# Moving the partner features of a rotary embedding between partitions by DMA instead of by a TensorE product

## The reference, cut to what matters

```
kh = axial_rope(rms_norm_2(kb..., g_knorm), ang_row, ang_col)
qh = axial_rope(rms_norm_2(qb..., g_qnorm), ang_row, ang_col)

def rotate(x, ang):                    # on each half of the 128 features
    x1, x2 = x[..., :m], x[..., m:]    # m = 32
    return concatenate([x1 * cos - x2 * sin, x2 * cos + x1 * sin])
```

## Time and profile before

| what | value |
|---|---|
| median of 3 runs | 3807.99 us (3806.25 to 3811.59) |
| profiled execution, its own time | 3809.24 us |
| its span | 3807.1 us |
| PE busy | 3518.0 us (92% of the span) |
| DVE, ACT, POOL busy | 1419.5, 991.5, 781.9 us |
| preparation of heads, group 0 | about 2371 to 2471 us of the span |
| preparation of heads, group 1 | about 2671 to 2774 us of the span |

### The profile page before, as it was taken

The page is one execution under the profiler, slowest core; times in us unless marked ns, Lnnn a source line. Parts: engine busy times, 40 slices in busy tenths (PEclk is TensorE's granted clock), DMA queues, the critical chain, the costliest instruction groups (busy, mean ns, idle before and its releaser), DMA issues.

```text
span 3807.1 us, 54098 instructions
## 1 busy us (share of the span) xinstructions
PE 3518.0 (92%) x20966; PEld 3032.4 (80%) x20966; DVE 1419.5 (37%) x2330; ACT 991.5 (26%) x1723; POOL 781.9 (21%) x515
## 2 busy tenths in 40 slices
PE   8999988999999989999999999899999999699996
PEld 6666766888887868888888899777777999489996
DVE  3454343000004545555555520645555133511212
ACT  3232241000001224444444410244144211311112
POOL 3112203232322332111111132100100122012121
PEclk9999989999999999999999999999999999799998
DMA  3001112111112120000000011100000121468786
GB/s 144 23 22 33 33 56 78 50 44 50 44 49 89 50 84 18 17 19 25 17 17 17 11 42 58 68 1 11 23 1 11 55 90 56 157 232 274 267 271 220
DMA packets 69590, 268.89 MB, mean 71 GB/s; under 512 B 9249, under 2 KB 9889, under 8 KB 68753
## 3 DMA queue, kind: packets, MB, share of 16 engines
q1 hardware_dynamic: 62304, 228.81, 17.3%
q0 software_dynamic: 5632, 17.05, 2.0%
q10 hardware_dynamic: 1584, 22.07, 1.4%
HBM read 229.55 MB, written 38.34 MB: 70 GB/s over the span
## 4 chain that ended last, share of the span: by engine, by line
PE 54%; DVE 4%; issue 2%; ACT 1%; DMA 0%; POOL 0%; ACTq 0%; DVEq 0%; POOLq 0%; SPq 0%
PE PS L511 23%; PE PS L499 6%; PE PS L2207 6%; PE PS L2096 4%; PE PS L2215 3%; PE PS L1950 3%; PE PS L1909 3%; PE PS L2075 3%; PE PS L2097 1%; PE PS L1951 1%; DVE EA L1586 1%; PE PS L2019 1%; PE PS L2062 1%; PE PS L2024 0%; PE PS L1922 0%
## 5 line engine op out<-in xcount | busy, mean ns | idle before, releaser
L511 PE MATMUL PS<-u_hi,w_hi 128*128 128x512 f32 (+1 forms) x2464 | 661.4, 363 | 39.9 <-DVE u_lo L465 11.5
L511 PE MATMUL PS<-u_lo,w_hi 128*128 128x512 f32 (+1 forms) x2464 | 653.5, 360 | 0.0
L511 PE MATMUL PS<-u_hi,w_lo 128*128 128x512 f32 (+1 forms) x2464 | 648.7, 358 | 0.0
L533 POOL CAST w_hi<-ring 128x1024 fp32r<-128x1024 f32 x174 | 183.0, 1052 | 1805.0 <-PE PS L511 1608.9
L511 PEld LDWEIGHTS PS<-u_hi,w_hi 128*128 128x128 f32 x2464 | 439.0, 190 | 114.5 <-issue 51.5
L511 PEld LDWEIGHTS PS<-u_hi,w_lo 128*128 128x128 f32 x2464 | 441.6, 189 | 57.1
L511 PEld LDWEIGHTS PS<-u_lo,w_hi 128*128 128x128 f32 x2464 | 443.0, 189 | 54.1
L535 POOL TENSOR_TENSOR w_lo<-ring,w_hi 128x1024 fp32r<-128x1024 f32 x174 | 419.6, 2411 | 14.0
L904 DVE TENSOR_TENSOR hid<-sq,PS 128x1024 f32 x22 | 26.9, 1221 | 457.9 <-PE PS L511 457.9
L1349 ACT ACTIVATE EA<-EA,small_sb 128x1040 f32<-128x1040 f32 x144 | 166.4, 1155 | 90.2 <-DVE small_sb L1586 90.1
L1586 DVE CUSTOM_DVE_ANT_0 EA<-PS,biasH,low_a 128x1024 f32<-128x1024 f32 x128 | 163.4, 1281 | 25.8 <-PE PS L1909 25.1
(11 more groups left out here) (332 smaller groups left out, 5274.3 us busy)
## 6 DMA issues: line engine op xcount, KB each, us to landing
ring<-in_stream SPq DMA_DIRECT2D x174, 512.0 KB, 3.5
w_gate_sb<-in_w_gate SPq DMA_DIRECT2D x64, 512.0 KB, 3.9
w_up_sb<-in_w_up SPq DMA_DIRECT2D x64, 512.0 KB, 7.1
w_down_sb<-in_w_down SPq DMA_DIRECT2D x64, 512.0 KB
x_keep<-xT ACTq DMA_DIRECT2D x2, 4176.0 KB, 13.0
xT<-x_keep ACTq DMA_DIRECT2D x1, 4176.0 KB, 12.9
x2T<-x_keep ACTq DMA_DIRECT2D x1, 4176.0 KB, 14.0
x_keep<-x2T SPq DMA_DIRECT2D x1, 4176.0 KB, 13.8
```

The costliest lines, as they stand in the source:

```text
L511: last = mm(bank(to_bank, width), w[j][:, c, :], src[:, c, b * width:(b + 1) * width], start=(c == 0 and k == 0), stop=(c == KD - 1 and k ...
L533: pool.tensor_copy(w_hi[j][:, :, :], w_raw[j][:, :, :]).then_inc(S["w_rounded"], 1)
```

## The change

The permutation matrix `swap`, its load and its product are gone. In their place ACT starts four DMAs a head, SBUF to SBUF, 32 partitions by 1040 floats (130 KB) each, which write the partner rows of `raw_b` straight into `swapped`. The sign that `swap` carried is now in the table `sin`.

- ACT starts them behind the square of the head, when `raw_b` is written and DVE has finished the last product of the head before (`ob_q`), which is the last reader of `swapped`. The wait stands in ACT's program ahead of `root(n)` and `raw(n+1)`.
- `ob_sw` now counts the landed DMAs (64 a head). DVE's product with the sine waits for it, and is one instruction on 1040 elements from SBUF instead of three from PSUM. `raw(n)` waits for it as before.
- The waits on `ob_m2` that guarded the PSUM banks, ahead of the next projection and of the second square root, are gone.

```
-    swap = np.zeros((P, P), np.float32)
...
+    for first in (0, 64):
+        sin[first:first + 32] *= -1.0
...
-                sp.dma_start(swap[:, :], A["swap"]).then_inc(S["const_ld"], 16)
...
-                pe.wait_ge(S["const_ld"], 48)
+                pe.wait_ge(S["const_ld"], 32)
...
-                            act.wait_ge(S["ob_sw"], i)
+                            act.wait_ge(S["ob_sw"], 64 * i)
                         act.activation(thirds(raw_b[:, :]), banks(3 * (n % 2), 3, CH), ACT.Copy, scale=gain).then_inc(S["ob_raw"], 1)
                         act.activation(thirds(sq_b[:, :]), banks(3 * (n % 2), 3, CH), ACT.Square).then_inc(S["ob_sq"], 1)
+                        act.wait_ge(S["ob_raw"], i + 1)
+                        if i >= 1:
+                            act.wait_ge(S["ob_q"], i)
+                        for r in range(0, P, 32):
+                            act.dma_start(swapped[r:r + 32, :], raw_b[r ^ 32:(r ^ 32) + 32, 0:T2]).then_inc(S["ob_sw"], 16)
...
-                        act.wait_ge(S["ob_m2"], 3 * i + 3)
...
-                        dve.wait_ge(S["ob_sw"], i + 1)
-
-                        for k in range(3):
-                            w = min(CH, T2 - k * CH)
-                            c = slice(k * CH, k * CH + w)
-                            if i and k == 0:
-                                dve.wait_ge(S["ob_m3"], i)
-                            ins = dve.tensor_tensor(swapped[:, c], bank(3 * (n % 2) + k, w), sin[:, c], ALU.mult)
-                            ins.then_inc(S["ob_m2"], 1)
-                        dve.wait_ge(S["ob_m2"], 3 * i + 3)
+                        dve.wait_ge(S["ob_sw"], 64 * (i + 1))
+                        dve.tensor_tensor(swapped[:, :], swapped[:, :], sin[:, :], ALU.mult).then_inc(S["ob_m2"], 1)
+                        dve.wait_ge(S["ob_m2"], i + 1)
...
-                        for b in range(3):
-                            last = mm(bank(first + b, CH), swap[:, :], raw_b[:, b * CH:(b + 1) * CH], start=True, stop=True)
-                        last.then_inc(S["ob_sw"], 1)
...
-                            pe.wait_ge(S["ob_m2"], 3 * (i - 1))
...
-                    pe.wait_ge(S["ob_m2"], 3 * (z0 + GROUP))
```

More of the change, by code:

```diff
@@ L84, in host_constants @@
     block = np.kron(np.eye(2), np.ones((HD, HD))).astype(np.float32)
-    swap = np.zeros((P, P), np.float32)
-    for half in (0, 64):
-        for i in range(32):
-            swap[half + 32 + i, half + i] = -1.0
-            swap[half + i, half + 32 + i] = 1.0
     delta = np.arange(P)[:, None] - (np.arange(T1)[None, :] - (T1 - P))
@@ L108, in host_constants @@
     sin = np.sin(ang).astype(np.float32)
-    return {"eye": eye, "ones": ones, "block": block, "swap": swap, "log_count": log_count, "neg_dist": neg_dist,
+    for first in (0, 64):
+        sin[first:first + 32] *= -1.0
+    return {"eye": eye, "ones": ones, "block": block, "log_count": log_count, "neg_dist": neg_dist,
             "cos": cos, "sin": sin}
@@ L148, in build @@
         block64 = put("block_sb", [P, P])
-        swap = put("swap_sb", [P, P])
         gains = put("gains_sb", [P, GAINS])
```

## The result

| | before | changed |
|---|---|---|
| median, 20 runs each | 3808.19 us | 3825.80 us |
| lowest and highest run | 3795.05, 3821.36 | 3811.28, 3838.57 |
| ratio, with its 95% interval | | 1.0037 (1.0024 to 1.0051) |
| profiled execution, its own time | 3809.24 us | 3826.91 us |

The ratio times the time before is 14 us more; 10 less were forecast. Times in us.

What follows compares the result with a forecast made beforehand. PE was taken as the bound, with a 16.82 us head period and DVE's chain close at group ends. Gains of 4.7 and 5.7 us, 10.4 together, off the median of 3807.99 gave 3798 us, range 3795 to 3807.

Steps and rivals of the forecast that it cites:

- The product with `swap` off PE: In each pipeline head PE loses 1.85 us of matmul, so its period falls from 16.82 to 14.97 us.
- The issue: Four DMA starts on ACT, 0.48 us apart, hold ACT about 1.9 us a head, hidden behind PE's projection.
- The landing: L, from DVE's last product of one head to its next sine product: taken as 4.0 us, bounds 3.44 and 5.84.
- the prediction's own formula: Total gain is 10.4 - 2 x (L - 4.0) up to L = 4.47, then 9.5 - 8 x (L - 4.47).
- The rival of slow narrow transfers: 32-partition transfers at half rate, one after another: L = 5.3, gain 2.9, total 3805 us; chance 22%.
- the estimate of 4.8: L from the skill page's 189 GB/s: some 2.8 us plus a fixed 2, a gain near 7.
- DVE's cycle: Per head on DVE, L + 10.5 us, 14.5 at L = 4.0, so under PE's 14.97, which sets the pace.
- The sign that I had named for it: The forecast is wrong if DVE's reciprocal starts behind its own sum, as DVE's cycle is then the pace.
- The end of a group: Scores start 0.1 us behind `k_lo`, gaining 4.7 and 5.7 us in the two groups; PE idle 5 to 7 us before.
- PE's clock: Rival: longer idling ahead of the scores doubles the low-clock stretch there, losing 6.4 us in all; total 3804; chance 8%.
- The chances: Faster 0.60, same within 0.2% 0.33, slower 0.07.
- a late landing: Rival: DVE waits for the DMAs in every head; slower from L = 5.66 (10%), by over 0.2% from 6.6.

Runs made afterwards that it cites:

- a_dbl: The changed kernel with a second buffer for the partner rows, so a head's DMAs wait for the head before the last; 3808.52 us, ratio 0.9969 against before.
- a_poolwait: The changed kernel with POOL's split of the next weights held until DVE has made the sum; 3810.12 us, ratio 1.0001 against before.

## Why the prediction was wrong

- *The product with `swap` off PE.* Right in itself: 60 records gone. The pace of 14.97 us came only where DVE let it: 15.04 in a_dbl and 15.02 to 15.04 in a_poolwait.
- *The issue.* Taken as 0.48 us apiece, measured 0.54 to 0.64 (1.40 and 1.21 in the first four). Hidden on ACT's side, as forecast, but for 0.8 us in head 4: its copy waited for the landing of head 3's transfers, where PE was no longer waited for.
- *The landing.* Taken as 4.0, measured 4.28 to 4.33 in seven of eight intervals and 5.15 in the last of group 1, which cost the scores there some 0.8 us; why is not known. One transfer lands in 2.4 us (2.2 assumed from the 64 and 512 KB rows). By the prediction's own formula the 0.28 costs 0.6 us. The rival of slow narrow transfers (L = 5.3 in every head) is out, and so is the estimate of 4.8 from the Trainium skill's page SBUF — State Buffer, section "Door 1: The DMA port swizzle".
- *DVE's cycle.* This step failed in its size. I put three operations at 1.24 us each, from rows in which POOL was still. With L at 4.28 DVE's cycle was 14.8 and just under PE's; the stretch by POOL, 2.55 us in head 1 and 1.45 in head 2, made it the pace. a_poolwait takes this out: its preparations are 3.0 and 3.9 us shorter than the changed kernel's (the late landing in group 1, 0.8 us, did not come again there either), 6.9 of the 8.0 us by which the changed stage missed its forecast (a gain of 2.4 for 10.4; of 9.3 in a_poolwait). The sign that I had named for it, a reciprocal that starts behind its own sum and not behind the root, is in the period of the chain shown above.
- *The end of a group.* Right: the scores 0.11 us behind `k_lo`, PE idle for 5.45 and 7.55 us, where 5 to 7 were forecast.
- *PE's clock.* This step decided the result, and it failed in its place and its size. I gave the clock 8% and 6.4 us, at the scores alone. The row at the scores did become lower than in the earlier trace rows, 0.50 for 7 us, as that rival said:

```profile
2459.00:2466.00 7.00, 7.00 (x26) 6.25 (x27) 2.14 (x7) 0.00 (x0) 0.00 (x0) 0.50 0.00 0
```

  The rest fell in the 200 us of attention behind it, where I took the clock as fixed because nothing changed there. The term should have read: 52 us more at the low level, at 0.38, minus 20 us. What brings these 52 us about is open but for the pauses that they follow. The kernel before already showed how wide this can be: its 20 runs went from 3795 to 3821, almost three times my gain.
- *The chances.* "Slower" came from a late landing only, with 7%. A cost that can fall on any change that shifts a loop by a microsecond was in none of the cases. Nothing in the trace of before gave its sign, but it did show that the attention's time was not fixed: its two attentions run the same instructions and took 200.2 and 204.5 us, with 6.5 and 17 us at the low level.

## What to carry to other kernels

Where runs of one kernel scatter by 20 us or more with their mean clock, split every result into the time at full clock and the low-clock time, by a fit of span against clock over all runs, and hold the first against the stages, since low-clock time in which PE waits anyway costs nothing. A gain under 0.5% is hard to tell otherwise, and a few versions with a harmless shift of a microsecond show how much of a loss the clock can make by itself. A transfer that replaces matmuls needs its own buffer: with one buffer the landing and all that stretches DVE stand in the loop (up to 17.28 us a head here, 15.04 with two), and an operation that moves from PSUM to SBUF operands is to be priced beside what POOL does there.

## What the runs showed of the hardware

- A transfer from SBUF to SBUF of 32 partitions by 1040 floats (130 KB), on ACT's queue, landed in 2.4 us in the median (2.2 to 3.3, but 6.0 to 6.7 for the four that were started while the store of 4176 KB was under way); four that were started 0.6 us apart had landed 4.2 us after the first start in eight of nine cases, and 5.0 in the other.
- A DVE operation and a POOL operation that both read two SBUF operands of some 1000 elements took 3.30 and 3.25 us side by side; alone they took 1.24 and 2.4. The one that began later was the one drawn out: in a_poolwait DVE's cosine product began at 2675.44, 0.08 us ahead of POOL's subtraction, and took 1.24 us, POOL's 3.41.
- With the granted clock at 0.50 PE went on without a gap; over an attention each us at the low level cost 0.41 us, and 0.38 over whole runs, not the 0.5 of lost work. Low-clock time in the preparations, where PE was ahead of DVE, cost nothing (87.0 us with 11.5 us of it and with 3.4).
- Two products of 256 columns, run once a group, gave a median of 3826 us and four of them 3807, beside 3817 without any. In 14 profiles all 82 falls of the clock inside an attention stood within 7.3 us behind a pause of PE of over 1.2 us. I had not expected that the clock in a loop of 200 us depends so finely on when the loop starts.
